# Expert gate and up weights of a hybrid decoder step: one block and one 1 MB transfer each, with one wait, in place of interleaved halves

## The chip, the cores and the metric

One Trainium2 chip, one of its cores. The metric is the device time of one execution in microseconds, as the median of several runs. Everything is float32 except the small one-hot matrices with which tokens are selected (bfloat16).

## What is computed

One layer for 512 prompt tokens and 8 sample tokens of width 1024: a modulated RMS norm, a mixer (retention and pooling), then a mixture of experts with 64 routed experts and one shared expert, of which each token takes eight. The part that matters here is the expert layer:

```python
hg = jnp.einsum('td,edf->tef', t, w_eg)
hu = jnp.einsum('td,edf->tef', t, w_eu)
a = jax.nn.silu(hg) * hu * gates.astype(t.dtype)[:, :, None]
routed = jnp.einsum('tef,efd->td', a, w_ed)
shared = jnp.dot(jax.nn.silu(jnp.dot(t, w_sg)) * jnp.dot(t, w_su), w_sd)
return routed + shared
```

t has 520 rows (d = 1024), f is 256. So each expert has a gate and an up matrix of 1024 x 256 and a down matrix of 256 x 1024, 1 MB each. The gates are zero for the experts that a token does not take, so only the tokens that took an expert need its matrices.

## The kernel before, in words

Everything is in one SBUF arena, and the waits between engines are written out by hand on semaphores.

Before the experts come the modulation rows, the mixer and the routing (up to about 390 us). Then the kernel works through items. An item is one expert with up to 128 of its tokens; an expert with more tokens gets a second item from a list that VectorE makes at run time. The shared expert runs first, as five items over the five token tiles (`shared_gu`, L959), with its weights in `sh_gu` and `sh_dn`.

One item w has these steps, and the engines work at several items at once:

- VectorE chooses (`choose`, L1635 to L1642): it reads the item's expert and first slot from the list into registers and makes the one-hot matrix of the item's tokens. TensorE multiplies it (`select`, L1013 to L1022) to get the token numbers, and VectorE writes these as indices (L1650, L1651).
- GpSimd gathers the token rows (`gather`, L603 to L612) from `h2_rows` in HBM. TensorE transposes them (`x_transposes`, helper at L708), ScalarE copies them to `xgT` (L1233).
- TensorE multiplies them with gate and up in one accumulation of 8 contraction tiles, 512 columns wide, 256 of gate and 256 of up (`gate_up`, L928 to L934). It comes in two parts of four contraction tiles each.
- ScalarE and VectorE form the activation a (L1210, L1561, L1565). TensorE transposes it (`a_transposes`, L942) and multiplies by down (`down`, L945 to L957). ScalarE and VectorE copy the result to `Y` (L1226, L1576).
- GpSimd scatters `Y` with addition into `moe_sums` in HBM (`scatter`, L614 to L625). A scatter waits for the one before it to land (L618), as two of them may add to the same row. VectorE's `keep_rows` (L1663 to L1667), which frees the index buffer, waits for a scatter as well, and `choose` for a later item stands behind it on VectorE. The order there is `y_copy` (L1576), `keep_rows` (L1667), `choose` (L1640, L1642).

TensorE's order within an item (`item`, L1030 to L1049) is: gate and up part 0 of item w, select of item w + 2, the transposes of a of the item before, gate and up part 1 of w, x transposes of w + 1, down of the item before. A float32 product of 128 x 512 shows as two records in the trace, so each part is 8 records of L933 and a down product is 8 records of L955.

The weights are loaded by SyncE's queue (`load_item`, L500 to L506), in the order of the list, into four sets of buffers (q = w mod 4). Before it loads item w it waits until item w - 4 is through with the buffer: `s_gh` (part 0 done) for the first half of the contraction tiles, `s_gm` (part 1 done) for the second, `s_dm` (down done) for the down matrix. As down of an item comes one item later on TensorE, the queue does `load_down` of item w - 1 right before it comes to gate and up of item w.

An item's gate and up buffer has the layout [contraction tile k, 512]: gate in columns 0 to 255 and up in columns 256 to 511 of each k. `load_gate_up` (L490 to L495) moves one half (k = 0 to 3 or 4 to 7) of gate and then of up, 512 KB each, four in all, with one semaphore per half (`s_guw[q][half]`). Row p x 8 + k of a matrix is contraction row k of partition p, so that in HBM a partition's eight rows of 1 KB lie side by side; in the arena they lie 2 KB apart. TensorE waits for the first half ahead of part 0 (L1034) and for the second ahead of part 1 (L1041).

The down buffer of an item is [2, 1024], and one transfer of 1 MB fills it (L498): 8 KB per partition, side by side in HBM and in the arena.

## Time and profile before

| | |
|---|---|
| median of 3 runs | 1246.63 us (1244.76 to 1246.88) |
| span of the profiled execution | 1243.9 us |
| that execution's own time | not given apart from its span; the median of the runs is 2.7 us above the span |
| TensorE busy (matmul) | 1150.2 us, 92% |
| VectorE, ScalarE, GpSimd busy | 396.0, 245.0, 218.6 us |
| moved by DMA | 305.82 MB in 200623 packets |
| expert loop | about 420 to 1197 us |
| after it | about 47 us: last scatters, residual, final norm, output |

A row of the timeline gives the start in us from the span's start, the duration, the engine, the line and the operation; rows that follow each other on one line are merged (x8), and the last record's modelled end is in the duration, so the time that a group takes is read from its start to the start of the next. The clock that was granted to TensorE is 1.00 (of 2.4 GHz) in the loop. For DMAs, q1 is the hardware queue (SyncE's transfers) and q0 the software queue (GpSimd's gathers and scatters); their share is that of the time of 16 DMA engines, and can go a little above 100% in a short window, as packets that reach over its end count in full. "To landing" is the time from the issue of a DMA to its semaphore.

### The profile page before, as it was taken

Reading aid. Unit: us, or ns where it says so; the run is one execution under the profiler, and the core shown is the slowest. Engines: PE = TensorE matmul, PEld = TensorE weight load, DVE = VectorE, ACT = ScalarE, POOL = GpSimd, SP = SyncE. Lnnn points to the kernel's source line nnn. Section 1 sums busy time; section 2 is a strip of 40 time slices with the busy share of each in tenths; the row PEclk is TensorE's granted clock in tenths of the full one; section 3 lists DMA queues with packets and bytes.
Section 4 is the critical chain, followed back from the end, with each engine's and each line's share of the span. In section 5 each row is a group of like instructions: output and inputs, shape, how many; then the busy total and the mean of one; then the engine's idle time right before and its main releaser. Section 6 shows DMA issues by size and latency. Waiting matters only on the chain. (4 is left out here: it accounts for less than half of the span.)

```text
span 1243.9 us, 14302 instructions
## 1 busy us (share of the span) xinstructions
PE 1150.2 (92%) x4176; PEld 588.9 (47%) x4176; DVE 396.0 (32%) x1070; ACT 245.0 (20%) x505; POOL 218.6 (18%) x175
## 2 busy tenths in 40 slices
PE   3799998999988999999999999999999999999960
PEld 0477454444544444544544544544544544444430
DVE  3533345424355222222222222222222222222226
ACT  1400101101101212212212212212212212122114
POOL 0000700000000122222222222222222221222214
PEclk9699998589989999999999999999999999999985
DMA  9963004330466899999999999999999999999613
GB/s 295 404 212 91 3 1 156 133 131 34 172 196 212 287 308 320 329 328 311 312 309 293 304 311 290 307 300 322 319 341 302 315 310 301 310 305 312 191 20 137
DMA packets 200623, 305.82 MB, mean 246 GB/s; under 512 B 18507, under 2 KB 165019, under 8 KB 191621
## 3 DMA queue, kind: packets, MB, share of 16 engines
q1 hardware_dynamic: 180694, 271.31, 65.0%
q0 software_dynamic: 19904, 34.18, 10.9%
q8 instruction: 15, 0.25, 0.1%
q14 instruction: 10, 0.08, 0.0%
HBM read 300.41 MB, written 43.50 MB: 276 GB/s over the span
## 5 line engine op out<-in xcount | busy, mean ns | idle before, releaser
L933 PE MATMUL bank<-arena 128*128 128x512 f32 x1152 | 521.0, 594 | 1.4 <-ACT arena L1233 1.4
L933 PEld LDWEIGHTS bank<-arena 128*128 128x128 f32 x1152 | 213.7, 191 | 245.4 <-issue 243.3
L955 PE MATMUL bank<-arena 128*128 128x512 f32 x576 | 262.2, 598 | 4.2 <-ACT arena L1216 4.2
L622 POOL DMA_INDIRECT moe_sums<-arena x68 | 107.5, 1582 | 514.8 <-issue 440.4
L955 PEld LDWEIGHTS bank<-arena 128*128 128x128 f32 x576 | 104.5, 191 | 110.8 <-issue 107.3
L1576 DVE COPY arena<-bank 128x512 f32<-128x512 f32 x72 | 49.9, 693 | 208.5 <-PE bank L955 208.5
L1561 DVE TENSOR_TENSOR arena<-arena,bank 128x256 f32<-128x256 f32 x72 | 30.4, 422 | 257.8 <-ACT arena L1210 257.7
L708 PEld LDWEIGHTS bank<-arena 128*128 128x128 f32 x632 | 84.5, 193 | 46.5 <-issue 34.7
L610 POOL DMA_INDIRECT arena<-h_rows,arena x70 | 71.8, 1026 | 180.9 <-DVE arena L1651 180.1
L708 PE MATMUL bank<-arena 128*128 128x128 f32 x632 | 86.8, 282 | 7.0 <-DVE arena L1333 6.2
L1640 DVE TENSOR_TENSOR arena<-arena 128x640 bf16 (+1 forms) x71 | 59.3, 835 | 70.5 <-issue 70.5
L1233 ACT ACTIVATE arena<-bank 128x512 f32<-128x512 f32 x138 | 75.0, 596 | 34.4 <-PE bank L708 34.4
L1226 ACT ACTIVATE arena<-bank 128x512 f32<-128x512 f32 x72 | 43.1, 598 | 184.9 <-PE bank L955 180.1
L1216 ACT ACTIVATE arena<-bank 128x256 f32<-128x256 f32 (+1 forms) x73 | 27.9, 382 | 230.5 <-PE bank L942 227.2
L1210 ACT ACTIVATE arena<-bank 128x256 f32<-128x256 f32 x72 | 27.7, 385 | 227.5 <-PE bank L933 227.5
L728 PE MATMUL bank<-arena 128*128 128x260 f32 x256 | 59.1, 391 | 0.4 <-issue 0.4
L903 PE MATMUL bank<-arena 128*128 128x512 f32 x128 | 58.2, 614 | 0.4 <-DVE arena L1416 0.4
L751 PE MATMUL bank<-arena 128*128 128x512 f32 x128 | 57.5, 593 | 0.5 <-issue 0.5
L728 PEld LDWEIGHTS bank<-arena 128*128 128x128 f32 x256 | 49.2, 194 | 11.8 <-issue 3.1
L675 PE MATMUL bank<-arena 128*9 128x512 f32 x192 | 30.5, 768 | 15.2 <-DMA arena<-in_w_ada 15.2
L903 PEld LDWEIGHTS bank<-arena 128*128 128x128 f32 x128 | 24.9, 197 | 31.5 <-issue 31.5
L1021 PEld LDWEIGHTS bank<-arena 128*128 128x128 bf16 x350 | 18.1, 96 | 44.4 <-issue 29.3
(214 smaller groups left out, 661.9 us busy)
## 6 DMA issues: line engine op xcount, KB each, us to landing
arena<-in_w_exp_gate SPq DMA_DIRECT2D x136, 512.0 KB
arena<-in_w_exp_up SPq DMA_DIRECT2D x136, 512.0 KB
arena<-in_w_exp_down SPq DMA_DIRECT2D x68, 1024.0 KB, 10.4
arena<-in_w_ada SPq DMA_DIRECT2D x12, 2048.0 KB, 11.1
arena<-in_w_in SPq DMA_DIRECT2D x2, 4096.0 KB, 23.2
arena<-in_w_out SPq DMA_DIRECT2D x1, 4096.0 KB, 19.8
arena<-in_x_prompt SPq DMA_DIRECT2D x4, 512.0 KB, 12.8
h_rows<-arena SPq DMA_DIRECT2D x4, 512.0 KB, 8.5
```

Of the source, the lines that this page charges most:

```text
L610: pool.indirect_dma_start(out=xg[:, par, :], out_offset=None, in_=h2_dram, in_offset=bass.IndirectOffsetOnAxis(ap=gidx[:, par:par + 1], ax ...
L622: pool.indirect_dma_start(out=sums, out_offset=bass.IndirectOffsetOnAxis(ap=sidx[:, par:par + 1], axis=0), in_=Y[:, (par + NT) % 2, :], in ...
L708: ins = pe.transpose(b[:, k % 4, :], sv[:, k, :], ident[0:rows, 0:rows])
L728: ins = mm(bank[GB[i % 4]][:, 0:HALF], w_gu[:, k, n * P:(n + 1) * P], hT[:, k, f * HALF:(f + 1) * HALF], start=(k == 0), stop=(k == KD - 1))
L751: ins = mm(bank[b + f][0:R, :], hT[:, k, tcols(t)], w_qkv[:, k, f * 512:(f + 1) * 512], start=(k == 0), stop=(k == KD - 1))
L903: ins = mm(bank[b + f][0:R, :], catT[:, k, tcols(t)], w_out[:, k, f * 512:(f + 1) * 512], start=(k == 0), stop=(k == KD - 1))
L933: ins = mm(bank[gb][0:R, :], xT[k], wts[:, k, :], start=(k == 0), stop=(k == KD - 1))
L955: ins = mm(bank[2 + f][0:R, :], aT[:, par, k, 0:R], wts[:, k, f * 512:(f + 1) * 512], start=(k == 0), stop=(k == 1))
L1226: A(Y[0:R, par, 0:512], bank[2][0:R, :], ACT.Copy).then_inc(s_ya, 1)
L1233: ins = A(xgT[par][:, 4 * i:4 * i + 4, :], bv(4 + i, 4, P), ACT.Copy)
L1576: V.tensor_copy(Y[0:R, par, 512:1024], bank[3][0:R, :]).then_inc(s_yb, 1)
L1640: c.do(TT(sel[par], iota[:, ds(base, P)].unsqueeze(1).broadcast_to([P, NT, P]), posm[:, :, ds(e, 1)].broadcast_to([P, NT, P]), ALU.is_equal))
```

## The change

The gate and up buffer of an item gets the layout [2, k, 256]: all of gate (8 KB per partition), then all of up. Each is loaded by one transfer of 1 MB, both count on one semaphore per buffer, and TensorE waits for it once, ahead of part 0. SyncE's wait for part 0 (`s_gh`) goes, and with it the semaphore. The moving operand of a product is then two runs of 256 columns that lie 8 KB apart, in place of one run of 512. The shared expert's gate and up get the same layout (they were loaded by one transfer each already), and the products for its last tile of 8 rows are written out in place of the helper.

```diff
--- before.py
+++ after.py
@@ -243,9 +243,9 @@
 
 
 
-        gu_w = [view(a, (KD, 512)) for a in (W, W + 4096, hT_at, mod_at)]
+        gu_w = [view(a, (2, KD, EF)) for a in (W, W + 4096, hT_at, mod_at)]
         dn_w = [view(W + 8192 + i * 2048, (2, D)) for i in range(4)]
-        sh_gu = view(W + 12288, (KD, 512))
+        sh_gu = view(W + 12288, (2, KD, EF))
         sh_dn = view(W + 16384, (2, D))
         squares = view(M, (D,))
         wo_g = view(M + D, (2, 512))
@@ -351,8 +351,7 @@
         s_xT, s_xTs, s_gm, s_sg, s_a = sem("xT_done"), sem("xT_in_sbuf"), sem("gate_up_done"), sem("gate_sigmoid"), sem("a_ready")
         s_aT, s_aTs, s_dm, s_ya, s_yb = sem("aT_done"), sem("aT_in_sbuf"), sem("down_done"), sem("y_left"), sem("y_right")
         s_sca, s_ysh = sem("scattered"), [sem("shared_stored0"), sem("shared_stored1")]
-        s_guw = [[sem(f"gate_up{i}_in{j}") for j in range(2)] for i in range(4)]
-        s_gh = sem("gate_up_half")
+        s_guw = [sem(f"gate_up{i}_in") for i in range(4)]
         s_dnw = [sem(f"down_in{i}") for i in range(4)]
         s_yin = [sem(f"sums_in{i}") for i in range(NT)]
         s_x3, s_fs, s_fv, s_fsd, s_out = (sem(n) for n in ("x3", "x3_squares", "x3_var", "x3_std", "out_rows"))
@@ -472,7 +471,7 @@
             sp.wait_ge(s_store, 16 * 8)
             sp.dma_start(w_rt, I["w_router"][0].rearrange("(p k) e -> p k e", k=KD)).then_inc(s_rt, 16)
             for i, name in enumerate(("w_sh_gate", "w_sh_up")):
-                sp.dma_start(sh_gu[:, :, i * EF:(i + 1) * EF],
+                sp.dma_start(sh_gu[:, i],
                              I[name][0].rearrange("(p k) f -> p k f", k=KD)).then_inc(s_shw, 16)
             sp.dma_start(sh_dn, I["w_sh_down"][0].rearrange("(p k) n -> p k n", k=2)).then_inc(s_shw, 16)
 
@@ -484,24 +483,22 @@
                     load_ada(10)
                     load_ada(11)
 
-            eg = [I[n][0].rearrange("e (p k) f -> p e k f", k=KD) for n in ("w_exp_gate", "w_exp_up")]
+            eg = [I[n][0].rearrange("e (p k) f -> p e (k f)", k=KD) for n in ("w_exp_gate", "w_exp_up")]
             ed = I["w_exp_down"][0].rearrange("e (p k) n -> p e k n", k=2)
 
-            def load_gate_up(e, q, half):
-
-                k = slice(4 * half, 4 * half + 4)
+            def load_gate_up(e, q):
+
                 for i in range(2):
-                    sp.dma_start(gu_w[q][:, k, i * EF:(i + 1) * EF].unsqueeze(1),
-                                 eg[i][:, ds(e, 1), k]).then_inc(s_guw[q][half], 16)
+                    sp.dma_start(gu_w[q][:, i].rearrange("p k f -> p (k f)").unsqueeze(1),
+                                 eg[i][:, ds(e, 1)]).then_inc(s_guw[q], 16)
 
             def load_down(e, q):
                 sp.dma_start(dn_w[q].unsqueeze(1), ed[:, ds(e, 1)]).then_inc(s_dnw[q], 16)
 
             def load_item(w, e, q):
 
-                for half in range(2):
-                    sp.wait_ge(s_gm if half else s_gh, w - 4 + NT + 1)
-                    load_gate_up(e, q, half)
+                sp.wait_ge(s_gm, w - 4 + NT + 1)
+                load_gate_up(e, q)
                 sp.wait_ge(s_dm, w - 4 + NT + 1)
                 load_down(e, q)
 
@@ -512,14 +509,12 @@
 
             sp.wait_ge(s_adam, NCH)
             for w in range(2):
-                for half in range(2):
-                    load_gate_up(w, w, half)
+                load_gate_up(w, w)
             store_shared(0)
 
             sp.wait_ge(s_h2, NT)
             sp.wait_ge(s_bcs, 10)
-            for half in range(2):
-                load_gate_up(3, 3, half)
+            load_gate_up(3, 3)
             store_shared(1)
 
             sp.wait_ge(s_table, 1)
@@ -528,8 +523,7 @@
                 load_down(w, w)
 
             sp.wait_ge(s_gm, NT)
-            for half in range(2):
-                load_gate_up(2, 2, half)
+            load_gate_up(2, 2)
             store_shared(3)
             load_down(2, 2)
             load_down(3, 3)
@@ -928,10 +922,13 @@
             def gate_up(n, xT, wts, R, gb, part):
                 for k in range(4 * part, 4 * part + 4):
                     if R == NS:
-                        ins = sample_product(gb, xT[k], wts, P, k, KD - 1)
+                        for j in range(4):
+                            ins = mm(bank[gb][32 * j:32 * j + NS, 0:P], xT[k], wts[:, j // 2, k, j % 2 * P:(j % 2 + 1) * P],
+                                     start=(k == 0), stop=(k == KD - 1), tile_position=(0, 32 * j))
                         continue
-                    ins = mm(bank[gb][0:R, :], xT[k], wts[:, k, :], start=(k == 0), stop=(k == KD - 1))
-                ins.then_inc(s_gm if part else s_gh, 1)
+                    ins = mm(bank[gb][0:R, :], xT[k], wts[:, :, k, :], start=(k == 0), stop=(k == KD - 1))
+                if part:
+                    ins.then_inc(s_gm, 1)
 
             def a_transposes(n, R, par):
                 pe.wait_ge(s_a, n + 1)
@@ -1031,14 +1028,13 @@
 
                 n, par = w + NT, q % 2
                 pe.wait_ge(s_xTs, w + 1)
-                pe.wait_ge(s_guw[q][0], (w - q) * 8 + 32)
+                pe.wait_ge(s_guw[q], (w - q) * 8 + 32)
                 pe.wait_ge(s_a, n - 1)
                 xT = [xgT[par][:, k, :] for k in range(KD)]
                 gate_up(n, xT, gu_w[q], P, (par + NT) % 2, 0)
                 select(w + 2, par)
                 R = ROWS[4] if first else P
                 a_transposes(n - 1, R, (par + NT - 1) % 2)
-                pe.wait_ge(s_guw[q][1], (w - q) * 8 + 32)
                 gate_up(n, xT, gu_w[q], P, (par + NT) % 2, 1)
                 x_transposes(w + 1, 1 - par)
                 if first:
```

## Rows read from the trace of the kernel before

**Rows 1.** Windows: busy us by engine, PEclk, DMA share, GB/s
```profile
450.00:1160.00 710.00, 707.82 (x2368) 350.86 (x2368) 183.31 (x604) 149.00 (x304) 158.15 (x122) 1.00 0.98 311
```

**Rows 2.** Timeline of TensorE over one item: start us, us
```profile
805.56 3.60 PE L955 MATMUL bank<-arena 128*128 128x512 f32 x8
...
812.44 0.27 PE L1021 MATMUL bank<-arena 128*128 128x6 bf16 x5
...
816.33 1.05 PE L708 MATMUL bank<-arena 128*128 128x128 f32 x8
817.21 3.60 PE L955 MATMUL bank<-arena 128*128 128x512 f32 x8
```

**Rows 3.** The same timeline: the first and last down products of the 67 items
```profile
420.50 3.60 PE L955 MATMUL bank<-arena 128*128 128x512 f32 x8
...
1193.83 3.60 PE L955 MATMUL bank<-arena 128*128 128x512 f32 x8
```

**Rows 4.** The chain that ended last, from 1093 us: start us, us, what
```profile
1093.12 10.73 DMA moe_sums<-arena
...
1103.87 0.07 DVE arena L1667
...
1106.64 0.28 PE bank L1021 x5
```

**Rows 5.** Timeline of VectorE over an undisturbed item
```profile
809.80 0.14 DVE L1667 COPY arena<-arena 128x1 int32<-128x1 int32 x1
...
821.46 0.14 DVE L1667 COPY arena<-arena 128x1 int32<-128x1 int32 x1
```

**Rows 6.** Timeline of GpSimd: the scatter of that item
```profile
810.92 1.58 POOL L622 DMA_INDIRECT moe_sums<-arena  x1 [7.52 <-issue]
```

**Rows 7.** Landing of the loop's 62 scatters, issued from 437 to 1152 us
```profile
DMA to landing us min/median/max: 7.3/9.7/11.0
```

**Rows 8.** The page's part 1: the span
```profile
span 1243.9 us, 14302 instructions
```

**Rows 9.** The waits of SyncE's queue, from 430 to 1160 us
```profile
SPq L498 <- PE bank L955: 117.4, 48, 8.6
```

**Rows 10.** Landing of the down weights issued from 585 to 613 us
```profile
DMA to landing us min/median/max: 11.6/12.1/12.1
```

**Rows 11.** The page's DMA lines: all packets by size
```profile
DMA packets 200623, 305.82 MB, mean 246 GB/s; under 512 B 18507, under 2 KB 165019, under 8 KB 191621
```

**Rows 12.** The page's DMA issues: the down loads
```profile
arena<-in_w_exp_down SPq DMA_DIRECT2D x68, 1024.0 KB, 10.4
```

**Rows 13.** DMA of 426.0 to 427.5 us, only packets of 8 KB and over
```profile
q1 hardware_dynamic: 68, 0.56, 92.0%
```

**Rows 14.** DMA of 588.5 to 590.0 us, only packets under 2 KB
```profile
q1 hardware_dynamic: 556, 0.55, 109.4%
```

**Rows 15.** DMA of 600 to 700 us
```profile
q1 hardware_dynamic: 19531, 27.52, 84.4%
```

**Rows 16.** Landing of the last 3 scatters, 1180 to 1210 us
```profile
DMA to landing us min/median/max: 6.0/6.0/6.0
```

**Rows 17.** Landing of the 5 scatters issued from 425 to 475 us
```profile
DMA to landing us min/median/max: 9.1/9.3/9.6
```

**Rows 18.** DMA of 594 to 598 us, while a scatter of that stretch moves
```profile
DMA packets 808, 1.05 MB, mean 263 GB/s; under 512 B 168, under 2 KB 707, under 8 KB 787
```

**Rows 19.** Landing of the 5 scatters issued from 565 to 615 us
```profile
DMA to landing us min/median/max: 10.0/10.4/10.6
```

**Rows 20.** Timeline of TensorE: down products in that stretch
```profile
560.43 3.60 PE L955 MATMUL bank<-arena 128*128 128x512 f32 x8
...
619.11 3.60 PE L955 MATMUL bank<-arena 128*128 128x512 f32 x8
```

**Rows 21.** Groups from 430 to 1160 us: weight loads by line
```profile
L933 PEld LDWEIGHTS bank<-arena 128*128 128x128 f32 x994 | 184.1, 190 | 209.3 <-issue 209.3
...
L708 PEld LDWEIGHTS bank<-arena 128*128 128x128 f32 x504 | 65.9, 191 | 30.3 <-issue 30.3
```

## The prediction

> **What bounds the kernel now.** I read the windows first, then TensorE's timeline, then the chain, then the DMA rows. In the windows the reader is to see two numbers that both look like a bound: TensorE busy for 707.82 of 710 us at full clock, and the DMA engines at a share of 0.98 [rows 1]. The timeline separates them. Down to down, an undisturbed item takes 817.21 - 805.56 = 11.65 us, with no gap between its groups [rows 2]: TensorE sets the pace, and the DMAs are just about fast enough. The first and the last of 67 down products lie 773.33 us apart [rows 3], 66 items; 66 x 11.65 = 768.9, so 4.4 us are lost somewhere in the loop.
>
> The chain shows where. A scatter issued at 1093.12 lands 10.73 us later; `keep_rows` (L1667) starts 0.02 us behind the landing, `choose` follows, and select (L1021) comes at 1106.64 [rows 4]. In an undisturbed item L1667 is at 809.80 and select at 812.44, 2.64 us, without a stall on TensorE [rows 2, 5]; here it is 2.77 us from an L1667 that came late. So the second bound is the **landing of the scatter**. The scatter issued at 810.92 [rows 6] has until the next L1667 at 821.46 [rows 5], that is 10.54 us. The loop's scatters land in 7.3 to 11.0 us, median 9.7 [rows 7]. There is only about 0.8 us to spare on the median, and the change alters what a scatter shares the DMA engines with.
>
> The sum is made against the profiled execution, whose span is 1243.9 us [rows 8]. The median of the runs, 1246.63, is 2.7 us more; I carry that difference over as it is, so every difference below is added to 1246.63.
>
> **The change part by part.**
>
> *SyncE's waits.* The queue's only wait on TensorE in the loop is that of L498, the down load: 48 times, 117.4 us in all [rows 9]. No row of L494 is there. The reason is in the order: gate and up of item w come right behind `load_down` of w - 1, which waits for down of w - 5, a product that TensorE does after both parts of w - 4. So `s_gh` and `s_gm` have passed by then, and dropping the first and holding the first half for the second costs 0. Behind the remaining wait stand only the two gate and up issues and the next down, as before.
>
> *SyncE's issues.* Two fewer per item. SyncE waits anyway (above), so 0; nothing of another kind is moved past anything.
>
> *TensorE's wait.* One wait per item goes. There is no gap for it to close: from select at 812.44 to the x transposes at 816.33 are 3.89 us [rows 2], of which part 1's 8 records take 3.44 and the five of select and the transposes of a the rest. So 0. The remaining one asks for both halves at part 0. Their transfers are issued just behind the down load at the end of item w - 4, three items or 35 us ahead of use, and the slowest landing of a weight load shown is 12.1 us [rows 10]. What covers it is those 23 us; 0.
>
> *Weight packets.* This is the part with an effect. Today gate and up are cut into 1 KB runs: 165019 of 200623 packets are under 2 KB, while 9002 are of 8 KB or more [rows 11], and the 68 down loads [rows 12], with 8 KB per partition in one run, account for 68 x 128 = 8704 of these. So the new layout should give 8 KB packets for gate and up too. From the shares: 1.5 us x 16 engines x 0.920 / 68 = 325 ns for 8 KB [rows 13], and 1.5 x 16 x 1.094 / 556 = 47 ns for 1 KB [rows 14], 376 for 8 of them. The 2 MB of an item go from 2048 x 47 / 16 = 6.0 us to 256 x 325 / 16 = 5.2 us of each engine: 0.8 us less per item of 11.65, or 7 points of the queue's 84.4% [rows 15]. The Trainium skill, "DMA: Bandwidth & Descriptors", "Why small descriptors are slow", gives a fixed cost of some three cycles per packet. By an estimate from that page it would be 280 against 259 cycles, 0.45 us per item; the measured packets say 0.8.
>
> *The scatter's landing.* Not shown directly, so bounded from both sides. Below: with no weight traffic a scatter lands in 6.0 us [rows 16]; with the stream of 1 KB packets and no backlog, 9.3 us [rows 17]. Above: the row-by-row count of rival 2, 11.5 us. The nearest row is a stretch of the loop in which the queue is behind, so that a down load lands 12.1 us after its issue [rows 10] and its 8 KB packets (808 - 787 = 21 in these 4 us [rows 18]) pass while the scatter moves. There the scatters take 10.4 us [rows 19]. I take 10.4, as after the change all of the stream has such packets. The backlog itself should go, which speaks for less; that there will be more 8 KB packets beside a scatter than those 21 speaks for more.
>
> What 10.4 costs is read in the same stretch: five items take 619.11 - 560.43 = 58.68 us [rows 20], 0.43 more than 5 x 11.65, or 0.09 per item. Over 66 items that is 5.7 us in place of the 4.4 lost today: **+1.3 us**.
>
> *The split moving operand.* Two runs of 256 columns per product. Nearest rows: 8 records of 512 columns take 3.44 us (812.44 less 805.56 for 16 of them), 430 ns each; 8 transposes of 128 columns take 817.21 - 816.33 = 0.88 us, 110 ns each [rows 2]. Between them a column costs 0.833 ns and a start 3.3 ns. If the second run cost as much as a new start, the 994 records of L933 [rows 21] would be 3.3 us longer, all of it on the path. Below, 0: nothing gets shorter. I take 0, because the weight loads of the transposes step 8 elements at a time and take 191 ns, those of L933 read a plain run and take 190 [rows 21].
>
> *Before and after the loop.* The shared gate and up were one transfer each already, on the same place in the queue, and behind the loop no gate or up is loaded: 0.
>
> Sum: +1.3. Forecast 1246.6 + 1.3 = **1247.9 us**.
>
> **The rivals.**
>
> *1. The relief wins.* With the queue 7 points lighter there is no backlog, and scatters land as in the stretch without one, 9.3 us [rows 17], or up to 10. None is late, the 4.4 us come back: 1246.6 - 4.4 = 1242.2 us. For it: lateness is found where the queue is behind. Against: those 9.3 us were had beside 1 KB packets.
>
> *2. The scatter becomes the bound (slower).* Place: the software queue's rows on the DMA engines, between weight packets. If one weight packet passes between two rows of a scatter, each row waits for 325 ns in place of 47, 278 more. 128 rows on 16 engines are 8 each (an even spread is assumed), so 2.2 us: 9.3 + 2.2 = 11.5. It decides from 10.54 us on: from there each item is as much longer as the scatter is later. In full it would be 1.0 us x 66 - 4.4 = +61 us, 1308 us; half way, at 10.9, +0.36 x 66 - 4.4 = +19, 1266 us, which is the value that I give it. For it: the scatter's steady neighbour will be 8 KB packets only. Against: in the stretch with such packets the landing grew by 1.1 us, not 2.2. The Trainium skill, same page, "Queues, rings and completion order", has the DMA engines take turns between queues packet by packet, which is a rule that speaks against this change. By that rule it is this rival in full; the 10.4 us agree with it only by half.
>
> *3. The split operand costs.* 3.3 us on top of the forecast: about 1251.2 us. For it: TensorE has no gap in which to hide it. Against: the transposes' strided loads.
>
> *4. The change doesn't do what it says.* The transfers are still cut to 1 KB and only issues and waits go. Then nothing happens: 1246.6. Against: the down loads.
>
> **How the numbers follow.** Two tenths of a per cent, 2.5 us, is about what a measurement of this kernel can tell from no change. The forecast has 0.34, rival 1 0.26, rival 2 0.24, rival 3 0.10, rival 4 0.06. Faster by over 0.2%: rival 1 and 0.03 of the forecast's own spread, 0.29. Slower: rival 2, most of rival 3, and 0.06 of the forecast's spread, 0.38. The rest, 0.33, is no change. Range: from a little below rival 1, 1241 us, to rival 2's half-way value, 1266 us; beyond it lies the fuller form of rival 2. Both signs hold much of the chance; the forecast's own range is 1245 to 1252.
>
> **What the profile after would show.** Right: q1's packets down by some 120 thousand and nearly none of 1 KB in the loop; the DMA share near 0.9; no L494 among SyncE's waits; 430 ns per L933 record; scatters landing in 10.0 to 10.8 us with several small waits of L1667. Rival 1 shows landings under 10 us and items of 11.65 throughout. Rival 2 shows items evenly longer, `moe_sums` ahead of L1667 in most of them, and TensorE idle before L1021. Rival 3 shows a longer L933 step with L955's unchanged. The forecast is wrong if the landing's median leaves 10.0 to 10.6 us, or if TensorE waits anywhere but before select.

## The result, and the profile after

The kernel with the change takes **1256.18 us** (median of 5 runs, 1252.88 to 1259.59); the kernel before took 1246.54 in 5 runs. The ratio is 1.0084, 95% interval 1.0064 to 1.0104: slower by about 9.6 us. The profiled execution after took 1259.59 us, the longest of the five, with a span of 1257.7, 13.8 more than before [rows 8]. So the profile shows a somewhat larger loss than the median.

The page after: span, packets, the weight queue, and the weight loads' issues (KB each, median us to landing).

```profile
span 1257.7 us, 13974 instructions
DMA packets 74798, 305.80 MB, mean 243 GB/s; under 512 B 16331, under 2 KB 21531, under 8 KB 48133
q1 hardware_dynamic: 54870, 271.31, 56.9%
...
arena<-in_w_exp_gate SPq DMA_DIRECT2D x68, 1024.0 KB, 7.2
arena<-in_w_exp_up SPq DMA_DIRECT2D x68, 1024.0 KB, 11.4
arena<-in_w_exp_down SPq DMA_DIRECT2D x68, 1024.0 KB, 4.8
```

The change did what it says. The same bytes move in 125825 fewer packets [rows 11]; a down load lands in 4.8 us in place of 10.4 [rows 12]; nothing is behind any more. The page before has this line for q1:

```profile
q1 hardware_dynamic: 180694, 271.31, 65.0%
```

And the windows of the loop after show it too (columns as in [rows 1]): the DMA share falls from 0.98 to 0.85. But TensorE, which had been busy for 707.82 us, is now busy for 702.36.

```profile
450.00:1160.00 710.00, 702.36 (x2332) 344.20 (x2331) 182.26 (x599) 146.21 (x298) 156.78 (x120) 1.00 0.85 307
```

Lighter DMA engines and a TensorE that stands more. An undisturbed item of the kernel after says that the item itself did not get longer:

```profile
802.66 3.60 PE L952 MATMUL bank<-arena 128*128 128x512 f32 x8
806.09 3.60 PE L929 MATMUL bank<-arena 128*128 128x512 f32 x8
809.53 0.27 PE L1018 MATMUL bank<-arena 128*128 128x6 bf16 x5
...
814.30 3.60 PE L952 MATMUL bank<-arena 128*128 128x512 f32 x8
```

814.30 - 802.66 = 11.64 us, the item of [rows 2]; the 8 records of L929 take 809.53 - 806.09 = 3.44 us, as before. What changed is the scatter's landing. This is the view of `moe_sums` on GpSimd for the scatters issued from 430 to 1170 us: who waited for a scatter (us, times), and the landing.

```profile
who waited for it (us, times):
...
  DVE arena L1663: 9.2, 23
...
DMA to landing us min/median/max: 8.9/10.7/11.8
```

Before, the same view had this line; the landing was 7.3/9.7/11.0 [rows 7].

```profile
  DVE arena L1667: 2.1, 3
```

The median scatter lands 1.0 us later and is past its 10.54 us; `keep_rows` (now L1663) waits for it 23 times in place of 3. Past 10.54 us are 40 of the 62 landings, where before they were 9 of 63.

Which ones they are goes with the number of tokens. A scatter has 128 slots, but only the slots that hold a token move a row of 4 KB. Counted in the trace of either kernel, the 68 scatters have 4160 such rows (520 tokens, eight experts each) and 4544 packets of 8 bytes, together 68 x 128; the median scatter of the loop has 57 rows before and 56 after. The 40 late ones of the kernel after carry 77 rows on the mean, the other 22 carry 36.

The waits of TensorE and of SyncE's queue after (us in total, times, longest) show what that does and what else there is:

```profile
PE bank L1018 <- DVE arena L1638: 7.4, 18, 1.5
```

```profile
SPq L496 <- PE bank L952: 637.7, 62, 12.0
```

TensorE waits in the loop for one thing only, `choose` ahead of select, 18 times. It never waits for a weight. SyncE has 637.7 us of waiting in place of 117.4 [rows 9], and no wait on L492.

One late item in full, from the timeline after. A scatter is issued at 487.94, 1.15 us behind the last item's gate issue:

```profile
486.21 0.33 SPq L496 DMA_DIRECT2D arena<-in_w_exp_down  x1
486.79 0.33 SPq L492 DMA_DIRECT2D arena<-in_w_exp_gate  x1
487.21 0.38 SPq L492 DMA_DIRECT2D arena<-in_w_exp_up  x1
487.94 1.58 POOL L616 DMA_INDIRECT moe_sums<-arena  x1 [7.58 <-issue]
...
499.79 0.15 DVE L1663 COPY arena<-arena 128x1 int32<-128x1 int32 x1 [1.23 <-DMA moe_sums<-arena]
501.77 0.83 DVE L1636 TENSOR_TENSOR arena<-arena 128x640 bf16 x1 [1.83 <-issue]
502.81 0.28 PE L1018 MATMUL bank<-arena 128*128 128x6 bf16 x5 [1.55 <-DVE arena L1638]
```

It lands 11.8 us later; `keep_rows` follows, `choose`, and TensorE stood for 1.55 us. The DMA view of 487.94 to 493 us, of 493 to 496 and of 496 to 499 (packets, MB, share of 16 engines) shows where the 11.8 us went: for five us nothing of the scatter moves and the queue of weights is at 95.6%; then its 88 rows go through beside what is left of the 3 MB. The software queue's packets (q0) are those of the scatter and, behind them, of the gather that was issued near 491 us.

```profile
q1 hardware_dynamic: 260, 1.97, 95.6%
```

```profile
q1 hardware_dynamic: 98, 0.68, 56.8%
q0 software_dynamic: 89, 0.29, 46.4%
```

```profile
q0 software_dynamic: 169, 0.51, 50.8%
q1 hardware_dynamic: 55, 0.34, 28.7%
```

The first and the last full down product of the loop after:

```profile
423.14 3.60 PE L952 MATMUL bank<-arena 128*128 128x512 f32 x8
...
1207.40 1.88 PE L952 MATMUL bank<-arena 128*128 128x512 f32 x4
```

1207.40 - 423.14 = 784.26 us for 66 items, 10.9 more than the 773.33 of [rows 3]. Added up over the timeline, the step from the start of part 0 to select, 3.44 us when undisturbed, is longer by 12.2 us in all after and by 3.4 before: 8.8 of the 10.9. The records of select take 2.1 us more in all; all other steps of TensorE's item have their old length. Of the span's 13.8 us, 2.6 lie ahead of the loop (423.14 against 420.50) and 0.2 behind it. The first gather landed 9.8 us after its issue in place of 8.8, and TensorE waited for it 2.5 us in place of 0.8. Around and behind that wait the granted clock is at its lower level (0.50, that is 1.2 GHz) for longer. The window after, and the window before:

```profile
397.40:407.60 10.20, 7.12 (x14) 3.76 (x15) 0.00 (x0) 1.15 (x3) 0.17 (x1) 0.50 1.00 385
```

```profile
400.60:404.00 3.40, 3.29 (x4) 1.51 (x5) 0.00 (x0) 0.06 (x1) 0.00 (x0) 0.50 1.09 384
```

The second is all that there is at 0.50 between 390 and 420 us before. e1 and e2 below, with gate and up in 1 KB packets, have the same 10.2 us at 0.50 as the kernel after, so this part is not the work of the large packets.

### The profile page after: what moved, and what is told of

It is laid out like the page before. It is cut to its first block and busy times, and to the rows that moved or that the text cites. A ratio compares the mean times of both kernels' runs of the same rounds, so it can differ in the third digit from the quotient of the medians.

```text
span 1257.7 us, 13974 instructions
## 1 busy us (share of the span) xinstructions
PE 1157.5 (92%) x4176; PEld 587.8 (47%) x4176; DVE 397.3 (32%) x1070; ACT 245.0 (19%) x505; POOL 218.8 (17%) x175
## 3 DMA queue, kind: packets, MB, share of 16 engines
q1 hardware_dynamic: 54870, 271.31, 56.9%
q0 software_dynamic: 19904, 34.18, 10.9%
## 5 line engine op out<-in xcount | busy, mean ns | idle before, releaser
L929 PE MATMUL bank<-arena 128*128 128x512 f32 x1152 | 521.8, 594 | 1.4 <-ACT arena L1229 1.4
L929 PEld LDWEIGHTS bank<-arena 128*128 128x128 f32 x1152 | 212.7, 190 | 247.4 <-issue 245.0
L1572 DVE COPY arena<-bank 128x512 f32<-128x512 f32 x72 | 49.9, 693 | 208.8 <-PE bank L952 161.1
L1636 DVE TENSOR_TENSOR arena<-arena 128x640 bf16 (+1 forms) x71 | 58.8, 828 | 83.7 <-issue 83.7
## 6 DMA issues: line engine op xcount, KB each, us to landing
arena<-in_w_ada SPq DMA_DIRECT2D x12, 2048.0 KB, 11.8
```

Of the source, the lines that this page charges most:

```text
L929: ins = mm(bank[gb][0:R, :], xT[k], wts[:, :, k, :], start=(k == 0), stop=(k == KD - 1))
L1572: V.tensor_copy(Y[0:R, par, 512:1024], bank[3][0:R, :]).then_inc(s_yb, 1)
L1636: c.do(TT(sel[par], iota[:, ds(base, P)].unsqueeze(1).broadcast_to([P, NT, P]), posm[:, :, ds(e, 1)].broadcast_to([P, NT, P]), ALU.is_equal))
```

## The experiments

The theory after the result: **the 8 KB packets of the weights hold up the scatter's rows**, the landing passes its deadline, and `keep_rows` and `choose` carry that to TensorE. The rivals: the size of the transfers, the single wait or the layout with its split operand cost the time. Ratios are to the kernel before in the same job; its median lay between 1244.1 and 1246.5 us in the five jobs, so kernels of different jobs are compared by their ratios. The diffs show the lines that carry an edit and leave out the counts and arguments that follow from it. "66 items" is the time from the first to the 67th down product in the one profiled execution, 773.33 us before and 784.26 after; a late item is one of over 11.7 us, of which before has 10 and after 33.

**e1, one 1 MB transfer and one wait, but the old layout and so 1 KB packets** (on the kernel after):

```diff
-gu_w = [view(a, (2, KD, EF)) for a in (W, W + 4096, hT_at, mod_at)]
+gu_w = [view(a, (KD, 512)) for a in (W, W + 4096, hT_at, mod_at)]
-    sp.dma_start(gu_w[q][:, i].rearrange("p k f -> p (k f)").unsqueeze(1),
+    sp.dma_start(gu_w[q][:, :, i * EF:(i + 1) * EF].unsqueeze(1),
```

> The changed kernel with the old interleaved layout [k, 512], so that packets are 1 KB again; one 1 MB transfer per matrix and one wait per item stay. Theory P (the 8 KB packets delay the scatter, and nothing else of the change matters): time as before, 1246 us within 3, loop's scatters landing at a median near 9.7 us, DMA share of the loop near 0.98. Rival S (the size of the transfers and the single wait: all of an item's load is issued in one burst ahead of the scatter): as changed, 1256 us, landing near 10.7 us. Rival M (the split moving operand): as before too, but with 8 records of the gate and up line shorter than the 3.44 us that the changed kernel shows.

Measured 1245.66 us, ratio 0.9998 [0.9987, 1.0008]; 66 items in 771.14 us, 6 late. The packets and the landing of its scatters:

```profile
DMA packets 198445, 305.78 MB, mean 246 GB/s; under 512 B 16331, under 2 KB 162843, under 8 KB 189445
```

```profile
DMA to landing us min/median/max: 7.4/9.3/10.9
```

**e2, the new layout, the split operand and the one wait, but 1 KB packets** (each matrix by two transfers, of the even and of the odd k):

```diff
+for odd in range(2):
     for i in range(2):
-        sp.dma_start(gu_w[q][:, i].rearrange("p k f -> p (k f)").unsqueeze(1),
+        sp.dma_start(gu_w[q][:, i].rearrange("p (k b) f -> p k b f", b=2)[:, :, odd].unsqueeze(1),
```

> The changed kernel's block layout, split moving operand and single wait, but each matrix is loaded by two transfers of 512 KB, one of the even and one of the odd contraction tiles, so that no two 1 KB runs can be joined. Theory P: as before, 1246 us within 3, scatters landing near 9.7 us, some 190 thousand packets. Rival M (split operand): as changed, 1256 us. Rival S (single wait): as changed as well, landing near 10.7 us.

Measured 1246.42 us, ratio 1.0005 [0.9994, 1.0016]; 66 items in 771.58 us, 4 late, landing 7.8/9.6/10.9. With e1 this leaves only the packets: one transfer or two, one wait or two, the block layout and the split operand each make no difference that can be measured. Its first gather landed in 9.8 us, as late as in the kernel after, so that part of the entry is not the packets' of gate and up: TensorE waited 2.5 us for it, and the granted clock was 0.50 from 396.8 to 407.0 us, as in the kernel after.

**e3, the new layout in two transfers of k 0 to 3 and 4 to 7**, 4 KB packets:

```diff
+for half in range(2):
+    k = slice(4 * half, 4 * half + 4)
     for i in range(2):
-        sp.dma_start(gu_w[q][:, i].rearrange("p k f -> p (k f)").unsqueeze(1),
+        sp.dma_start(gu_w[q][:, i, k].rearrange("p k f -> p (k f)").unsqueeze(1),
```

> The changed kernel, each matrix loaded by two transfers of 512 KB, one of the first four and one of the last four contraction tiles: packets of 4 KB. Theory P with a delay in proportion to the packet: between the two, scatters landing near 10.1 us, 1248 to 1252 us. If two or more 1 KB packets already pass between two rows of a scatter, a 4 KB packet hardly costs more than these: 1246 us. Rival S: no difference from 8 KB, 1256 us.

Measured 1253.79 us, ratio 1.0068 [1.0051, 1.0086]; 66 items in 783.71 us, 26 late. The same view as above:

```profile
  DVE arena L1665: 9.4, 17
...
DMA to landing us min/median/max: 8.4/10.5/11.6
```

e2 and e3 differ in nothing but how the k are dealt to the two transfers. So the packet size costs the time. On the medians half the size costs four fifths of it, but the intervals of e3 and of the kernel after (1.0064 to 1.0104) overlap, so the two are not told apart; what was expected of a delay in proportion, 10.1 us and 1248 to 1252 us, was exceeded.

**e4, the kernel after with four index buffers**, so that `keep_rows` of item w needs scatter w - 4 and not w - 2. It takes away the wait of `keep_rows`, and leaves the weights and the scatter as they are:

```diff
-sidx = view(rt_at + 1046, (2,), I32)
+sidx = tiny((4,), I32)
-    dve.wait_ge(s_sca, (w - 1) * 16 + 16)
-V.tensor_copy(sidx[:, par:par + 1], midx[:, par:par + 1]).then_inc(s_sidx, 1)
+    dve.wait_ge(s_sca, (w - 3) * 16 + 16)
+V.tensor_copy(sidx[:, q:q + 1], midx[:, par:par + 1]).then_inc(s_sidx, 1)
```

> The changed kernel with four buffers for the scatter's indices in place of two: VectorE's copy of an item's indices then waits for the scatter four items back, not two, and so the choice behind it never waits for a late scatter. Packets stay at 8 KB. Theory P by way of this wait: scatters still land at 10.5 us or later, but no item is stretched, the loop's 66 items take 66 x 11.65 = 769 us in place of 784, and the time is 1256 - 10.9 - 4 = about 1242 to 1246 us (what stays is the later first gather, about 2.6 us). Rival Q (the late scatter holds GpSimd's next scatter and gather, and TensorE waits for the gather): no gain, 1256 us. Rival E (the time was lost ahead of the loop): no gain.

Measured 1243.64 us, ratio 0.9987 [0.9977, 0.9997]; no late item, 66 of them in 769.01 us, which is 66 x 11.65. Its windows, and its landing:

```profile
450.00:1160.00 710.00, 710.00 (x2379) 351.48 (x2378) 184.22 (x606) 150.02 (x305) 186.51 (x122) 1.00 0.86 313
```

```profile
DMA to landing us min/median/max: 6.1/10.6/11.1
```

The scatters are about as slow as in the kernel after, and TensorE is busy for all of 710 us. `y_copy` (L1572) still waits for a scatter, 11 times and 33.5 us in all, and that costs TensorE nothing. So the whole loss of the loop goes by the one wait of `keep_rows`; from a ratio of 1.0084 to 0.9987 some 12 us come back.

**e5, the same edit on the kernel before**:

```diff
-    dve.wait_ge(s_sca, (w - 1) * 16 + 16)
+    dve.wait_ge(s_sca, (w - 3) * 16 + 16)
```

> The kernel before (1 KB packets, halves, two waits) with four buffers for the scatter's indices. If late scatters cost the loop of before some 4.4 us by way of VectorE's copy of the indices, all 66 items now take 11.65 us and the time is 1245.7 - 4.4 = about 1241.5 us, some 2 us under the changed kernel with four buffers (1243.6), of which the rest is the later first gather. If those 4.4 us had another cause (the reads of the list into registers), the time stays at 1245.7.

Measured 1242.63 us, before 1244.1 in this job, ratio 0.9988 [0.998, 0.9997]; no late item, 769.12 us, landing 7.4/9.8/11.3. The 4.4 us that the kernel before lost in its profiled loop were such waits too: 4.2 of them are gone here. But each of these profiles is one execution. By the medians the gain is 1.5 us, where 4.4 were expected, so that most executions of the kernel before seem to lose less than the profiled one. With the wait gone, e4 and e5 stand level by their ratios (0.9987 and 0.9988): the larger packets then neither cost nor bring anything that can be measured.

**e7, the kernel after with down in two transfers of 512 columns**, 2 KB packets. If large packets ahead of the scatter do harm, fewer of them should help:

```diff
-sp.dma_start(dn_w[q].unsqueeze(1), ed[:, ds(e, 1)]).then_inc(s_dnw[q], 16)
+for f in range(2):
+    sp.dma_start(dn_w[q][:, :, f * 512:(f + 1) * 512].unsqueeze(1),
+                 ed[:, ds(e, 1), :, f * 512:(f + 1) * 512]).then_inc(s_dnw[q], 16)
```

> The changed kernel with the down matrix of an item loaded by two transfers of 512 KB, one per half of its columns, so that its packets are of 2 KB; gate and up stay at 8 KB. A third of the weight stream gets small packets, and it is the third that is served first, ahead of the scatter's rows. Theory P (a scatter row waits for whatever packet is beside it at that moment): no gain, 1254 to 1257 us, scatters landing near 10.6 us. Rival A (the mean packet size of the stream counts): a third of the way back, about 1252 to 1253 us.

Measured **1315.93 us**, ratio 1.0565 [1.0541, 1.0589]: a miss by 60 us. 66 items take 846.53 us. Landing, and TensorE's wait:

```profile
DMA to landing us min/median/max: 9.6/11.5/13.3
```

```profile
PE bank L1020 <- DVE arena L1640: 48.1, 36, 2.6
```

The median scatter lands at 11.5 us, 1.0 past the deadline, where that of the kernel after is 0.2 past it: now 41 of the 66 items are late, and the time is near that of rival 2 in full (1308 us). There is a second part. TensorE's timeline around one late item, and the windows of the stretch behind the wait:

```profile
488.71 0.28 PE L1020 MATMUL bank<-arena 128*128 128x6 bf16 x5 [1.75 <-DVE arena L1640]
488.91 0.47 PE L941 MATMUL bank<-arena 128*128 128x128 f32 x2
489.22 5.30 PE L931 MATMUL bank<-arena 128*128 128x512 f32 x8
```

```profile
489.20:494.40 5.20, 5.20 (x11) 2.17 (x10) 0.20 (x2) 0.39 (x1) 1.03 (x1) 0.67 1.02 359
494.40:498.70 4.30, 4.30 (x18) 2.38 (x17) 0.91 (x2) 1.47 (x3) 0.00 (x0) 1.00 0.65 227
```

Behind a wait of 1.75 us the granted clock is 0.67 on the mean over 5.2 us (0.50, that is 1.2 GHz, from 489.6 to 493.0 us), and 8 records take 494.36 - 489.22 = 5.14 us in place of 3.44. That happens in 11 items, behind waits of 1.73 to 2.55 us, and makes 18.2 us, added up over the timeline. In the kernel after, whose longest wait is 1.55 us, the 8 records of part 1 never take longer than 3.45.

Neither theory had this, so I formed another from the two timelines. The down load is issued at 483.55 us in e7, 3.3 us ahead of the scatter at 486.88, and gate and up behind it, still ahead of the scatter. The scatter's first row moves only some five us behind its issue. Of these five about three are the traffic's already: at the end of the loop of before and after, with no weights in the queue, the first row moves 2.1 to 2.3 us behind the issue. By then the small packets of down have passed, and what stands in q1 are the 8 KB packets of gate and up. The new theory: **what counts is what is left in q1 when the scatter's rows begin**, not what moves in the loop as a whole. The next runs were made to test it.

**e9, the kernel after with gate and up loaded ahead of down**: gate and up of item w wait for part 1 of item w - 4 alone and are issued without the down load ahead of them.

```diff
-sp.wait_ge(s_dm, w - 4 + NT + 1)
-load_down(e, q)
+sp.wait_ge(s_dm, w - 4 + NT)
+load_down(e_before, (q - 1) % 4)
```

> The changed kernel, with two index buffers and 8 KB packets as they are, but SyncE loads gate and up of item w before down of item w - 1: the wait for gate and up is passed at the end of part 1, some 4.3 us before the one for down, so that the 2 MB start 4.3 us earlier against the scatter and are mostly gone when its rows begin. Theory L: scatters land at 9.7 us or less, few or no items over 11.65 us, time 1243 to 1247 us. Rival A (packet size as such, wherever the packets stand): landing 10.7 us and 1256 us as before the reordering.

Measured 1243.76 us, ratio 0.9982 [0.9972, 0.9991]; 1 late item, 770.02 us. All weights still come in 8 KB packets. Timeline of the queue and GpSimd, the landing, and the DMA view from 489 to 492 us:

```profile
483.88 1.58 POOL L619 DMA_INDIRECT moe_sums<-arena  x1 [7.51 <-issue]
```

```profile
489.61 0.33 SPq L492 DMA_DIRECT2D arena<-in_w_exp_gate  x1
490.04 0.38 SPq L492 DMA_DIRECT2D arena<-in_w_exp_up  x1
493.80 0.33 SPq L496 DMA_DIRECT2D arena<-in_w_exp_down  x1
```

```profile
DMA to landing us min/median/max: 6.0/8.8/11.0
```

```profile
q0 software_dynamic: 194, 0.63, 79.8%
q1 hardware_dynamic: 23, 0.15, 16.0%
```

One gate load is issued at 477.96, 5.9 us ahead of the scatter, where it was 1.15 us ahead in the kernel after, and the next 5.7 us behind it; down is issued 1.7 us ahead (482.15). Between 489 and 492 us the software queue has the engines nearly alone: 194 packets in 3 us, of which 74 are rows of the scatter and 79 rows of the gather behind it; between 493 and 496 us in the kernel after it had 89, of which 64 and 7. It is the scatter of the same item, with 88 rows. Its first row moves 3.5 us behind the issue in place of 5.35, the last one 4.9 us behind the first in place of 5.6, and it lands in 9.0 us in place of 11.8. The median is 8.8. So it is not the 8 KB packets as such, it is their place in time. The same packets, 1.9 us less on the median: that is the new theory's, and the old one's no longer. But 1.1 of the 1.9 us are an earlier first row (3.8 us behind the issue in place of 4.9), which the theory does not speak of.

**e6, down in 2 KB packets on the kernel before** (the edit of e7):

```diff
+for f in range(2):
+    sp.dma_start(dn_w[q][:, :, f * 512:(f + 1) * 512].unsqueeze(1),
```

> The kernel before with the down matrix of an item loaded by two transfers of 512 KB, one per half of its columns (packets of 2 KB). The same edit to the changed kernel cost 60 us, with scatters landing at 11.4 us. Theory L (what counts is how many 8 KB packets are still left in the queue when the scatter's rows begin; a slower down load ahead of them leaves more): here only 1 KB packets stand behind the down load, so the time stays near the kernel before, 1244 to 1250 us, scatters landing at 9.5 to 10.3 us. Rival T (two down transfers cost this by themselves, by their issue or by a semaphore that comes late): 1300 us here too.

Measured 1241.75 us, before 1245.4, ratio 0.997 [0.9958, 0.9982]; 2 late items, 769.82 us, landing 7.2/8.7/10.6. The edit that costs 60 us in the kernel after gains some 3.7 in the one before, where 1 KB packets stand behind it. So rival T falls. Time and landing are both better than the 1244 to 1250 and 9.5 to 10.3 us that were expected; why is open.

**e8, e4 and the second down load held back until the first gather has landed**, and with it gate and up of item 2, which come behind it on the queue:

```diff
-for w in range(2):
-    load_down(w, w)
+load_down(0, 0)
+sp.wait_ge(s_gat[0], 16)
+load_down(1, 1)
```

> The changed kernel with four index buffers, and SyncE holding the down weights of item 1 and the gate and up weights of item 2 until the first gather has landed. Theory P for the entry to the loop: the first gather lands about 2 us earlier (near 7.5 us after its issue in place of 9.8), TensorE's wait for it (1.6 to 2.5 us) goes, and with a shorter cold stretch the time is 1.5 to 3 us under 1243.6. If the gather takes its 9 us for another reason, nothing changes.

Measured 1241.23 us, ratio 0.9977 [0.9966, 0.9987]. The first gather lands in 6.1 us in place of 8.9 in e4; the loop is the same, 769.01 us, and it begins 1.2 us earlier (first down product at 419.77 in place of 421.00). That is also what the ratios give, 0.9987 to 0.9977, but their intervals overlap, so the gain in time is not shown, and it is smaller than the expected 1.5 to 3 us.

**e10, the kernel after with e4, e8 and e9 together**:

```diff
-    dve.wait_ge(s_sca, (w - 1) * 16 + 16)
+    dve.wait_ge(s_sca, (w - 3) * 16 + 16)
-sp.wait_ge(s_dm, w - 4 + NT + 1)
+sp.wait_ge(s_dm, w - 4 + NT)
```

> The changed kernel with all three: four index buffers, first gather ahead of the weights of items 1 and 2, gate and up loaded before down. The loop has nothing more to give (e8 had every item at 11.65 us), so by theory L it stays at 1241 us within 1.5, with scatters landing well under 10 us. If it is faster by more, something else in the loop or at its end was still waiting for a transfer.

Measured 1241.53 us, ratio 0.9966 [0.9953, 0.9979]; 769.01 us, no late item, landing 5.3/8.7/10.5. Nothing that can be measured over e8: with the wait gone, the landing no longer matters.

**e11, e9 with down in 2 KB packets**: the edit that cost 60 us, but with gate and up ahead of down.

```diff
-sp.dma_start(dn_w[q].unsqueeze(1), ed[:, ds(e, 1)]).then_inc(s_dnw[q], 16)
+for f in range(2):
+    sp.dma_start(dn_w[q][:, :, f * 512:(f + 1) * 512].unsqueeze(1),
```

> The slow kernel of the down test (changed, down in two transfers with 2 KB packets, 1316 us) with gate and up of item w loaded before down of item w - 1, as in the reordered kernel. Theory L: the 8 KB packets are again mostly gone when the scatter's rows begin, and the 2 KB packets stand beside them: scatters land below 9.5 us, 1241 to 1246 us. Rival T (two down transfers beside 1 MB gate and up transfers are slow by themselves): most of the 60 us stay.

Measured 1240.01 us, before 1244.89, ratio 0.996 [0.9947, 0.9973]; 2 late items, 770.53 us. Landing:

```profile
DMA to landing us min/median/max: 7.7/9.4/11.4
```

From 11.5 us in e7 to 9.4, by the order of the loads alone. So the small packets of down did no harm by themselves.

The theory can be read in all of these traces. For every scatter of the loop I took its first row on the DMA engines, the rows of 4 KB in the 3 us from there, and what q1 moved in the same 3 us in packets of 4 KB and more; medians over 57 to 63 scatters each. The rows in the 3 us are all 4 KB packets of the software queue, so that rows of the gather behind the scatter are among them; the next column has the scatter's alone, told by their time (327 ns, a gather's 159).

| | first row behind issue, us | rows in 3 us | of these the scatter's | MB in large packets | landing, us |
|---|---|---|---|---|---|
| before | 5.0 | 59 | 48 | 0.06 | 9.7 |
| e2, 1 KB | 5.0 | 63 | 48 | 0.06 | 9.6 |
| e6, before with down 2 KB | 4.9 | 65 | 47 | 0.00 | 8.7 |
| after | 4.9 | 50 | 38 | 0.79 | 10.7 |
| e3, 4 KB | 5.2 | 44 | 40 | 0.72 | 10.5 |
| e7, after with down 2 KB | 5.3 | 45 | 37 | 0.80 | 11.5 |
| e9, gate and up first | 3.8 | 63 | 44 | 0.30 | 8.8 |
| e11, e9 with down 2 KB | 4.7 | 66 | 44 | 0.14 | 9.4 |

Where 0.7 to 0.8 MB of large packets pass beside the first rows, 44 to 50 rows get through, 37 to 40 of them the scatter's; where it is 0.3 or less, 59 to 66 do, 44 to 48 of them the scatter's. It orders the kernels into those that are slower and those that are not. It does not order the landings within the faster ones: e9 lands at 8.8 us beside 0.30 MB, the kernel before at 9.7 beside 0.06. Why e7 is 0.8 us worse than the kernel after at the same 0.8 MB is not in it: 0.4 us of that is the later first row, and the rest stays open.

**e12, the kernel before with four index buffers, down in 2 KB packets and the gather first** (the edits of e5, e6 and e8):

```diff
+for f in range(2):
+    sp.dma_start(dn_w[q][:, :, f * 512:(f + 1) * 512].unsqueeze(1),
+sp.wait_ge(s_gat[0], 16)
-    dve.wait_ge(s_sca, (w - 1) * 16 + 16)
+    dve.wait_ge(s_sca, (w - 3) * 16 + 16)
```

> The kernel before with what helped it: down in packets of 2 KB, four index buffers, and the down weights of item 1 and the gate and up weights of item 2 held until the first gather has landed. The loop is at its floor of 769 us in each of its parents, so what is left to gain is the entry: 1239 to 1242 us, against 1241.8 with 2 KB down packets alone.

Measured **1239.26 us**, ratio 0.9967 [0.9954, 0.998], the lowest median of the study, level with e11 (the intervals of the ratios overlap). Its windows:

```profile
450.00:1160.00 710.00, 710.00 (x2378) 353.41 (x2377) 185.63 (x610) 149.80 (x305) 184.92 (x122) 1.00 0.98 307
```

No late item, 769.12 us: what is left is TensorE's own work, at a DMA share of 0.98. Both e11 and e12 are faster than the kernel before, and so than the kernel after.

## Where the prediction was right, and the step that it mis-sized

The forecast was 1247.9 us; measured 1256.18. The sign is right, and "slower" had the largest of the three chances, 0.38. The time lies inside the range only by its end at rival 2's half-way value: the forecast's own range was 1245 to 1252 us. And the forecast fails by its own test: the landing's median was to stay within 10.0 to 10.6 us, and was 10.7. So the mechanism, a later scatter that `keep_rows` waits for, is the one that was named, and its size was wrong: + 1.3 us forecast, + 9.6 measured.

- **The step that was mis-sized is the scatter's landing, in both of its numbers.** The first: 10.4 us was taken from a stretch with 8 KB packets of down beside the scatter. Measured are 10.7, and 8.9 at the least (before 7.3). 0.3 us is not much, but the deadline of 10.54 lies between the two. The second: the price. 0.09 us per item came from that stretch; measured is (784.26 - 768.9) / 66 = 0.23. A mean over five items around a threshold says little of a distribution that has moved across it: 9 of 63 landings were past the deadline before, 40 of 62 after. e4 shows that this term is all of the loop's loss.
- **A late `keep_rows` costs more than its lateness.** Select comes 3.02 us behind it in the item above (502.81 - 499.79), and 2.64 when undisturbed. In between, VectorE stands 1.83 us before L1636 with nothing that the profile shows to wait for; in the two undisturbed items at 808 and 820 us it is 0.99 and 1.24 us. Why is open.
- **Rival 2 had the mechanism, at less than its half-way size**: + 10.9 us in the loop where it gave + 19, at a landing of 10.7 and not 10.9. By its own rule 10.7 gives 0.16 x 66 - 4.4 = + 6.2. Its full time is near that of e7, but not in its way: there 41 of 66 items are late, and 18.2 us are the lower clock. The even spread that it assumed, each item as much later, was seen nowhere; in the kernel after half of the items are undisturbed.
- **Its reason was incomplete.** It has one weight packet between two rows all the way. The rows of 493 to 496 us look like that, with 89 packets of the software queue to 98 of the weights'. But in the kernel before it is 207 to 626 between 816 and 819 us, while a scatter's rows move (71 rows of 4 KB are among the 89, and 52 among the 207; the rest are packets of 8 and 4 bytes):

```profile
q1 hardware_dynamic: 626, 0.62, 66.3%
q0 software_dynamic: 207, 0.21, 36.7%
```

The Trainium skill, "DMA: Bandwidth & Descriptors", "Queues, rings and completion order", has the engines take turns between queues packet by packet; if its packets are those of the profile, the first view agrees with equal turns and the second does not. e9 shows that the place of the weight packets in time matters, and e3 that 4 KB are nearly as bad as 8.
- **Its 8 rows per engine are too many.** The 2.2 us were worked out for 128 rows. The median scatter has 57, which is 3.6 per engine and by the same sum 3.6 x 278 ns = 1.0 us, and 1.0 us is what the median grew by. That agreement is an estimate's and may be luck: the same sum for 4 KB packets (159 ns each in e3 on the median, 112 more than 47) gives 0.4 us, and e3 has 0.8 to 0.9 over the kernel before and e2.
- **"The backlog goes" was right**, and rival 1 built on it was wrong. Down lands in 4.8 us, SyncE waits 520 us more, and the scatter came later all the same. A DMA share over 710 us does not tell what is in the queue in the six us in which the scatter moves.
- **Packets**: some 120 thousand fewer were expected, 125825 measured; share near 0.9, measured 0.85. The saving was undersized: 65.0% of 1243.9 us less 56.9% of 1257.7 is 92.9 us, over 68 items 1.4 us each, where 0.8 was worked out.
- **The steps costed at 0 were 0**: SyncE's waits (no L492 among them), its issues, TensorE's waits for weights (none), the shared expert. The **split operand** too: 3.44 us for 8 records, and e2 is level with before. So rival 3 falls, and rival 4 falls by the packet counts.
- **Not foreseen**: TensorE's entry into the loop, 2.6 us later. Ahead of it the granted clock is 0.50 for 10.2 us in place of 3.4, around and behind the wait for the first gather. The first gather's landing goes with what is loaded beside it: it lands in 8.7 to 9.9 us in the eight kernels with a 1 MB down load there, 1 KB packets of gate and up or not, in 5.5 to 7.6 in those with down in 2 KB packets (e6, e7, e11), and in 6.1 to 6.5 where weights are held back (e8, e10, e12). e1, e2 and e4 enter 1.1, 2.1 and 0.5 us later than the kernel before, e4 with the very loads of the kernel after. So little of the 2.6 us is shown to be the change's; how much is open.

## What to carry to other kernels

A transfer that runs beside a latency-bound one should be judged by what it leaves in the queue at the moment at which the other's rows begin, not by its packets' cost or by the mean load; a lighter queue made this kernel slower. Where a landing has a deadline, read its whole distribution against that deadline, and look first for the buffer that sets it: two more index buffers took the whole loss away, and the order of the loads did as much within the error. Count the rows that really move, too: the late scatters were those of the items with many tokens.

## What the runs showed that was not expected

- Packets of 4 KB delay a scatter nearly as much as those of 8 KB (landing 10.5 and 10.7 us), and those of 1 KB much less (9.3 to 9.7).
- A row of the scatter, which adds to what is there, takes 327 ns on its DMA engine, and a row of the gather, of the same 4 KB, 159.
- A third of the weights in smaller packets, issued ahead of the large ones, cost 60 us over the kernel after (e7); the same packets with the large ones ahead of them cost nothing (e11).
- In the loop the first row of a scatter moves 4.7 to 5.5 us behind its issue, on the median of each kernel; in the two kernels with gate and up first and 8 KB packets (e9 and e10) after 3.8 and 3.6. Without weights in the queue it is 2.1 to 2.3. Between the first and the last row lie 4.0 us before, 4.9 after and 5.2 in e7.
- Behind a wait of 1.75 us TensorE had a granted clock of 0.67 over the next 5.2 us; 11 items of e7 lost 18.2 us so, on top of the waits. The kernel before has a wait of 1.6 us, and none of its groups of 8 records there is longer than 3.45 us.
